# Fused transformer blocks on one core: joined products in a triangular inverse, a reordered tail, and SiLU ahead of a sigmoid

## The chip, the cores and the metric

The kernel runs as one launch on one core of a Trainium2 chip. The metric is the device time of a run in microseconds (us); lower is better. The core has five engines with a queue of instructions each: TensorE (PE in the rows; its weight loads are PEld), VectorE (DVE), ScalarE (ACT), GpSimd (POOL) and SyncE (SP), which here issues the DMAs. Everything is float32, and one matrix product of the program shows as two PE records in the trace. The engines meet only at semaphores that the program sets and waits for by hand.

## The reference, cut to what matters

The input is one sequence of 256 tokens of 1024 channels and 256 context tokens. Two layers of a first network are followed by one block of a second. The change touches only the second block:

```
u  = split(conv(modulate(x), modulate(ctx)) @ w_in)      # mq mk | r k v | mv mo | gates | low ranks
h_m = headnorm(mlstm(silu(mq), silu(mk), mv, gates)) * norm_w;  out_m = sigmoid(mo) * h_m
for t: state = state * w_t - (state @ kh_t) (kh_t a_t)^T + v_t k_t^T;  y_t = state @ r_t     # "wkv", two directions
out_r = (headnorm(y) + bonus) * g
x  = layernorm(ALPHA * x + g1 * ([out_m, out_r] @ w_out))
p  = softmax(h @ rt_g); group = argmax; two best experts of 8 in the group     # h = modulate(x), 32 experts
ffn = sum over the chosen: w * ((silu(h @ ex_gate[e]) * (h @ ex_up[e])) @ ex_down[e])
x  = layernorm(ALPHA * x + g2 * ffn)
```

## The kernel before

The program has six phases: `layers` (the first network), `mid` (projections, convolutions and the mLSTM), `wkv` (the recurrence), `tail` (output product, norms, router), `first` (the first block of an expert) and `pairs` (a loop over pairs of blocks of experts). PSUM has 8 banks. Each phase lists its groups of products in the order in which PE computes them (`wkv_groups`, `tail_groups`, `first_groups`), and the place in that list gives a group its bank and the counts with which `K.full` and `K.empty` are waited for. Each engine runs its queue in the order written in the functions below; nothing is scheduled by a planner.

End of `mid`: ScalarE (`mid_scalar`) takes the square roots of the key norms (L1564), drains the two banks `mo2` through a sigmoid (L1577, by `drain`, L1481), waits for the keys `kh`, and takes SiLU of `km` and `qm` in place (L1583, L1585). PE (`mid_tensor`) computes `mo2`, transposes the gates (L1394) and waits for `km` and `qm` before the first products of the mLSTM loop over four head pairs (`bG`, `qk`, `em`, L1239). That loop's exponentials are L1596 on ScalarE.

`wkv`: the 512 positions (256 of context, then 256 latents) are cut into 8 chunks c of 64; LAT = 4 is the first chunk with an output. Both directions z = 0, 1 run side by side, 8 heads each, as 8 products of 64 rows on the quadrants of the array. Per chunk and direction PE computes three products of the decayed keys (`mr`, `m`, `nr`, in `inner`, by the helper `each`, L1973), turns four operands by products with the identity (`t1`: b and k; `t2`: values and keys, L2001), and inverts a unit triangular matrix in six levels (`level`): a level squares the power and its transpose (`pw`, L2022) and multiplies the inverse by the power (`iv`, L1973). ScalarE copies `pw` (L2109), VectorE adds `iv` to the inverse (`grow`, L2211) and between two levels makes the decayed operands of the next chunk (`hats`, L2147 to L2150). Then come `nv`, `wu` (`solved`), and in the next chunk's turn `gr` (`moved`) and the outputs and state `y`, `st` (`outputs`). GpSimd fills constants for all this after `mid` is done (`wkv_tiles_gpsimd`, L2266, L2268).

`tail`: the output product has two token tiles of two halves of 512 columns, 8 products each: four with the mLSTM's channels, four with the recurrence's, which VectorE delivers one by one (`mixed_r`). `gate_rows(i)` turns a gate vector into rows (8 products L2315, two copies L2400). Per token tile VectorE does two layer norms with square roots on ScalarE (L2407, L2409), PE turns the tile (L2335), ScalarE modulates it (L2416), PE makes the router's logits (L2347), VectorE picks the experts (`route`) with exponentials on ScalarE. When both tiles are routed PE counts places (L2368 to L2379), and VectorE plans blocks of 64 places (`plan`): the number of blocks, the expert of each block (L2593 to L2601, which ends with the semaphore `planned`), and the place of each token.

`first` and `pairs`: the first block's expert is known early; its three matrices are loaded from L2304. `block_count` waits for `planned` and loads the number of blocks into a register. VectorE marks the tokens of the first block (`choose`), PE gathers them (L2667), then gathers the tokens of the next two blocks (L2658), then multiplies the first block with its gate and up matrices (L2681, L2682), turns the hidden rows (L2693), multiplies with the down matrix (L2702) and puts rows back (L2711). The loop over pairs starts at L2723; SyncE loads its weights, three matrices of 2 MB for each block, from `planned` on (L2638).

Of the kernel before, what the change touches and what calls it, by code (L numbers as in the profile page):

```python
# [1078 lines left out]
LAT = T // CH  # L1079


def wkv_groups():
    keys = []
    for c in range(CHUNKS + 1):
# [5 lines left out]
        for z in range(ZS):  # L1090
            if c < CHUNKS:
                keys += [("t1", c, z), ("t2", c, z)]
            if c > LAT:
                keys += [("y", c - 1, z)]
            if 0 < c < CHUNKS:
                keys += [("st", c - 1, z)]
        if c == CHUNKS:
            break
        for n in range(1, LEVELS + 1):
            for z in range(ZS):  # L1100
                if n < LEVELS:
                    keys += [("pw", n, c, z)]
                if n > 1:
# [11 lines left out]
def tail_groups():  # L1115
# [3 lines left out]
    return keys + [("pos", tt) for tt in range(TT)] + [("h2", tt, hf) for tt in range(TT) for hf in range(2)]  # L1119
# [52 lines left out]
CHUNK_EVENTS = dict(wkv_tiles=1, decay=CHUNKS * ZS, hats=CHUNKS * ZS, inv_start=CHUNKS * ZS)  # L1172
# [303 lines left out]
def mid_scalar(act, K):  # L1476
# [94 lines left out]
    key_norms((2, 3))  # L1571
    for i in range(2):
# [9 lines left out]
    act.wait_ge(K.sem["conv_mk"], K.count("conv_mk"))  # L1582
    act.activation(K.km, K.km, ACT.Silu).then_inc(K.sem["km"], 1)  # L1583
    act.wait_ge(K.sem["conv_mq"], K.count("conv_mq"))
    act.activation(K.qm, K.qm, ACT.Silu).then_inc(K.sem["qm"], 1)  # L1585
# [364 lines left out]

def by_pair(bank, n=P):
# [10 lines left out]
def wkv_tensor(pe, K):  # L1962

    one = K.one

# [14 lines left out]
    def inner(c, z):  # L1980
# [3 lines left out]
        kr = t.decayed(c, lat)  # L1984
        each(("mr", c, z), 2 if lat else 1, (t.b, kr))
        each(("m", c, z), 1, (t.decayed(c, False)[:, :, 0, :], t.b))
        each(("nr", c, z), 2 if lat else 1, (t.k, kr))

    def turned(c, z):

        t = K.wkv[z]
        at = chunk_at(c, z)
        v, kr = K.rv[:, :, at:at + CH], t.decayed(c, False)[:, :, 0, :]
        for name, two in (("t1", (t.b, t.k)), ("t2", (v, kr))):
            key = (name, c, z)
            pe.wait_ge(K.empty(key), K.empty_count(key))
            bank = by_two(K.bank(key))
            for i, src in enumerate(two):
                for u in range(HP):
                    for r in HEAD_ROWS:  # L2000
                        ins = pe.matmul(bank[r, u, i, :], src[r, u, :], one[r, :], start=True, stop=True)  # L2001
            ins.then_inc(K.full(key), 1)

    def level(n, c, z):
# [4 lines left out]
        if n == 1:  # L2009
            drained(("mr", c, z), ("m", c, z))  # L2010
        else:
            drained(("pw", n - 1, c, z))
        if n < LEVELS:
# [12 lines left out]
        elif n > 2:  # L2026
# [1251 lines left out]
```

## Time and profile before

| what | value |
|---|---|
| median of 3 runs (lowest, highest) | 2221.85 us (2221.75, 2222.93) |
| the profiled execution: time, span | 2219.88 us, 2218.1 us |
| mean granted TensorE clock | 0.967 of 2.4 GHz |
| busy: PE, DVE, ACT, POOL | 2077.0, 834.1, 480.6, 247.1 us |
| read from memory | 382.54 MB |
| start of `wkv` on PE, start of the output product, start of the loop over pairs | 1406.81, 1647.35, 1755.82 us |

A view of the profile gives times from the start of the span. In a timeline a row merges neighbouring instructions of one line: start, duration, engine, line, operation, operands, count, and in brackets how long the engine was idle before and what ended that. A PE record's duration includes its way through the array, so that neighbours overlap; what a stream of products costs is the distance between starts.

### The profile page before, as it was taken

Reading aid. Unit: us, or ns where it says so; the run is one execution under the profiler, and the core shown is the slowest. Engines: PE = TensorE matmul, PEld = TensorE weight load, DVE = VectorE, ACT = ScalarE, POOL = GpSimd, SP = SyncE. Lnnn points to the kernel's source line nnn. Section 1 sums busy time; section 2 is a strip of 40 time slices with the busy share of each in tenths; the row PEclk is TensorE's granted clock in tenths of the full one; section 3 lists DMA queues with packets and bytes.
Section 4 is the critical chain, followed back from the end, with each engine's and each line's share of the span. In section 5 each row is a group of like instructions: output and inputs, shape, how many; then the busy total and the mean of one; then the engine's idle time right before and its main releaser. Section 6 shows DMA issues by size and latency. Waiting matters only on the chain.

```text
span 2218.1 us, 36982 instructions
## 1 busy us (share of the span) xinstructions
PE 2077.0 (94%) x15231; PEld 1402.7 (63%) x15231; DVE 834.1 (38%) x1551; ACT 480.6 (22%) x868; POOL 247.1 (11%) x229
## 2 busy tenths in 40 slices
PE   8988999999998999999899999899996899999996
PEld 5776868864776777885355555799974444444342
DVE  1388220002248622000358846534446233233324
ACT  2245100000235400000132134443332011101110
POOL 1367000000057600000000001000000000000000
PEclk9999999999999999999899999899996899999998
DMA  7422534443533254444632324300012799999993
GB/s 233 152 76 95 190 120 152 152 153 127 174 120 108 95 190 134 152 153 151 215 109 76 113 92 140 115 4 4 4 43 114 290 372 393 394 412 394 392 393 157
DMA packets 138683, 385.63 MB, mean 174 GB/s; under 512 B 16903, under 2 KB 64367, under 8 KB 127409
## 3 DMA queue, kind: packets, MB, share of 16 engines
q1 hardware_dynamic: 138545, 383.61, 46.8%
q8 instruction: 109, 1.79, 0.3%
q14 instruction: 29, 0.24, 0.0%
HBM read 382.54 MB, written 1.05 MB: 173 GB/s over the span
## 4 chain that ended last, share of the span: by engine, by line
PE 41%; DVE 5%; ACT 2%; issue 1%; DMA 1%; DVEq 0%; POOL 0%; ACTq 0%; POOLq 0%
PE psum L1239 9%; PE psum L2723 9%; PE psum L1973 6%; PE psum L2747 4%; PE psum L2022 3%; PE psum L2658 3%; PE psum L2001 1%; PE psum L2326 1%; PE psum L1438 1%; ACT arena L1596 1%; DVE arena L2931 1%; DVE arena L2858 1%; PE psum L2735 1%; DMA ring<-in_w_ada_dram 1%; PE psum L1254 0%
## 5 line engine op out<-in xcount | busy, mean ns | idle before, releaser
L364 PE MATMUL psum<-arena,ring 128*128 128x256 f32 x1728 | 389.1, 385 | 17.2 <-DVE arena L935 15.8
L364 PEld LDWEIGHTS psum<-arena,ring 128*128 128x128 f32 x1728 | 330.0, 192 | 73.5 <-issue 16.6
L573 PE MATMUL psum<-arena,ring 128*128 128x256 f32 (+1 forms) x1536 | 306.8, 361 | 3.2 <-ACT arena L624 3.2
L573 PEld LDWEIGHTS psum<-arena,ring 128*128 128x128 f32 x1536 | 270.5, 189 | 39.3 <-ACT arena L624 4.0
L624 ACT ACTIVATE arena<-psum 128x512 f32<-128x512 f32 (+2 forms) x116 | 63.0, 568 | 541.1 <-PE psum L573 264.0
L1973 PE MATMUL psum<-arena 64*64 64x64 f32 (+1 forms) x3808 | 149.3, 228 | 6.4 <-DVE arena L2150 3.4
L600 PE MATMUL psum<-ring,arena 128*128 128x512 f32 x352 | 151.4, 592 | 0.0
L1973 PEld LDWEIGHTS psum<-arena 64*64 64x64 f32 x3808 | 139.3, 136 | 8.8 <-issue 3.6
L1239 PE MATMUL psum<-arena,ring 128*128 128x512 f32 (+2 forms) x432 | 142.2, 489 | 0.0
L1013 DVE TENSOR_TENSOR arena<-arena,psum 128x512 f32<-128x512 f32 x22 | 15.2, 690 | 288.8 <-PE psum L573 288.8
L600 PEld LDWEIGHTS psum<-ring,arena 128*128 128x128 f32 x352 | 66.9, 190 | 83.3 <-issue 83.2
L1239 PEld LDWEIGHTS psum<-arena,ring 128*128 128x128 f32 (+1 forms) x432 | 80.6, 187 | 61.4 <-issue 55.8
L2109 ACT ACTIVATE arena<-psum 128x512 f32<-128x512 f32 (+1 forms) x144 | 78.8, 553 | 145.3 <-PE psum L2001 65.1
L2723 PE MATMUL psum<-ring,arena 128*64 128x512 f32 x224 | 100.8, 603 | 4.3 <-DVE arena L2931 3.2
L2724 PE MATMUL psum<-ring,arena 128*64 128x512 f32 x224 | 100.8, 604 | 0.0
L2724 PE MATMUL psum<-arena 128*64 128x512 f32 x224 | 99.4, 595 | 0.0
L2723 PE MATMUL psum<-arena 128*64 128x512 f32 x224 | 99.3, 595 | 0.0
L2903 DVE TENSOR_TENSOR arena<-arena,psum 64x512 f32<-64x512 f32 x28 | 19.0, 679 | 211.9 <-ACT arena L2800 211.9
L1795 DVE SCALAR_TENSOR_TENSOR arena<-psum,arena 128x189 f32<-128x189 f32 (+3 forms) x184 | 80.5, 438 | 21.6 <-ACT arena L1535 13.2
L2800 ACT ACTIVATE arena<-psum 64x512 f32<-64x512 f32 x28 | 16.6, 594 | 310.6 <-PE psum L2724 310.6
L2022 PE MATMUL psum<-arena 64*64 64x64 f32 x2304 | 81.6, 218 | 0.8 <-issue 0.7
L992 DVE SCALAR_TENSOR_TENSOR arena<-arena,psum 128x512 f32<-128x512 f32 x16 | 11.0, 690 | 178.1 <-PE psum L600 135.9
(407 smaller groups left out, 2625.1 us busy)
## 6 DMA issues: line engine op xcount, KB each, us to landing
ring<-in_w_in_dram SPq DMA_DIRECT2D x31, 2048.0 KB, 8.3
ring<-in_ffn_w_dram SPq DMA_DIRECT2D x46, 1024.0 KB, 5.8
arena<-in_ex_gate_dram SPq DMA_DIRECT2D x15, 2048.0 KB, 11.2
arena<-in_ex_up_dram SPq DMA_DIRECT2D x15, 2048.0 KB, 15.7
arena<-in_ex_down_dram SPq DMA_DIRECT2D x15, 2048.0 KB, 17.4
ring<-in_ex_gate_dram SPq DMA_DIRECT2D x14, 2048.0 KB, 10.4
ring<-in_ex_up_dram SPq DMA_DIRECT2D x14, 2048.0 KB, 14.8
ring<-in_ex_down_dram SPq DMA_DIRECT2D x14, 2048.0 KB, 7.7
```

The lines of the kernel that those rows point to most:

```text
L364: ins = pe.matmul(bank[:, j, :], w[:, kc, c * P:(c + 1) * P], moving[:, kc, :], start=kc == 0, stop=kc == k - 1)
L573: ins = pe.matmul(bank[:, j, tokens], both[:, i * DC + kc, j * P:(j + 1) * P], K.xT[:, kc, tokens], start=kc == 0, stop=kc == DC - 1)
L600: ins = pe.matmul(banks[tt, hf], K.hT[:, kc, tt * P:(tt + 1) * P], w[:, i, hf * BANK:(hf + 1) * BANK], start=kc == 0, stop=kc == FC - 1)
L1239: ins = pe.matmul(out, a, b, start=i == 0, stop=i == len(pairs_) - 1)
L1795: last = stt(out=o, in0=i, scalar=w, in1=o, op0=ALU.mult, op1=ALU.add)
L1973: ins = pe.matmul(bank[r, u, :], a[r, u], b[r, u], start=i == 0, stop=i == len(terms) - 1)
L2022: ins = pe.matmul(bank[r, u, i, :], a[r, u], b[r, u], start=True, stop=True)
L2109: act.activation(dst, src, ACT.Copy).then_inc(K.empty(key), 1)
L2658: ins = pe.matmul(bank[:, u * P:(u + 1) * P], K.x_hat[:, tt, kc * P:(kc + 1) * P], K.chosen_at[:, tt, :], start=tt == 0, stop=tt == TT - 1)
L2723: pe.matmul(bank[0:PLACES, :], K.xg[:, kc, mine], up[:, kc, :], start=kc == 0, stop=kc == DC - 1)
L2724: ins = pe.matmul(bank[PLACES:P, :], K.xg[:, kc, mine], gate[:, kc, :], start=kc == 0, stop=kc == DC - 1)
L2747: ins = pe.matmul(bank[hf * PLACES:(hf + 1) * PLACES, :], K.p_hidT[:, j, kc, :], w[:, kc, hf * BANK:(hf + 1) * BANK], start=kc == 0, stop= ...
```

## The change

Five things change.

1. In `mid_scalar` SiLU of `km` and `qm` is taken before the two `mo2` drains, ahead of the wait for `kh`.
2. In `wkv` the values of all chunks are turned once, at the start (`vt`, 4 banks, 64 products), and copied back in place; `t2` is gone. `mr`, `m` and `nr` are products with 128 columns: beside the decayed keys stands the identity, so that the turned b, keys and k come out of the same products, and `t1` remains only for c >= LAT. GpSimd fills two more constants per direction.
3. In levels 2 to 4 (`JOINED`) the product of the power's transpose has power and inverse side by side as moving operand (`pw`, 128 columns), the square of the transpose is a product by itself (`pt`, 64 columns); ScalarE copies `pt`, and VectorE writes power and inverse in one addition of 512 elements per partition.
4. The tail's output product, gates, router counts and plan are reordered.
5. The first block's products with gate and up come before the gather of the next blocks; the experts of the blocks and the router's weights are computed after the first `choose`; `block_count` is read after the first block's work.

```diff
@@ mid_scalar
     key_norms((2, 3))
-    for i in range(2):
-        drain(("mo2", i), ..., ACT.Sigmoid, ...)
...
-    act.wait_ge(K.sem["kh"], K.count("kh"))
     act.wait_ge(K.sem["conv_mk"], K.count("conv_mk"))
     act.activation(K.km, K.km, ACT.Silu).then_inc(K.sem["km"], 1)
     act.wait_ge(K.sem["conv_mq"], K.count("conv_mq"))
     act.activation(K.qm, K.qm, ACT.Silu).then_inc(K.sem["qm"], 1)
+    for i in range(2):
+        drain(("mo2", i), ..., ACT.Sigmoid, ...)
...
+    act.wait_ge(K.sem["kh"], K.count("kh"))
@@ wkv_tensor: inner, level, start
-        kr = t.decayed(c, lat)
-        each(("mr", c, z), 2 if lat else 1, (t.b, kr))
-        each(("m", c, z), 1, (t.decayed(c, False)[:, :, 0, :], t.b))
-        each(("nr", c, z), 2 if lat else 1, (t.k, kr))
+        kr = t.decayed(c, True) if lat else t.decayed_and_one(c)
+        each(("mr", c, z), 2, (t.b, kr))
...
+                ins = pe.matmul(bank[r, u], t.decayed(c, False)[r, u, 0, :], t.b_and_one(u)[r], start=True, stop=True)
...
+        each(("nr", c, z), 2, (t.k, kr))
...
-        if n < LEVELS:
+        if n in JOINED:
+            each(("pt", n, c, z), 1, (z_now, zt_now))
+        elif n < LEVELS:
...
-        if n > 1:
+        if n in JOINED:
+            each(("pw", n, c, z), 2, (zt_now, t.power_and_inv(n - 1)))
+        elif n > 1:
             each(("iv", n, c, z), 1, (zt_now, t.inv))
...
+    pe.wait_ge(K.sem["one_ready"], K.count("one_ready"))
+    for i in range(CHUNKS // 2):
+        values_turned(i)
@@ tail_tensor, after the products
+    for key in (("pos", 0), ("pos", 1), ("total", 0)):
...
+    pe.wait_ge(K.sem["route"], K.count("route", 0, 1))
+    pe.matmul(pos0, K.earlier, K.chosen[:, 0, :], start=True, stop=True)
...
+    pe.wait_ge(K.sem["route"], K.count("route", 0, 2))
+    pe.matmul(total, K.ones, K.chosen[:, 1, :], start=False, stop=True).then_inc(K.full(("total", 0)), 1)
@@ wkv_vector: grow
-        tt_op(t.inv, t.inv, by_pair(K.bank(key), CH), ALU.add).then_inc(K.empty(key), 1)
+        if n in JOINED:
+            ins = tt_op(t.power_and_inv(n), by_two(K.bank(key)), t.zero_and_inv, ALU.add)
+        else:
+            ins = tt_op(t.inv, t.inv, by_pair(K.bank(key), CH), ALU.add)
+        ins.then_inc(K.empty(key), 1)
@@ wkv_tiles_gpsimd
     for t in K.wkv:
+        pool.memset(t.zero, 0.0).then_inc(link.sem, 1)
+        pool.wait_ge(link.sem, link.count())
+        pool.tensor_copy(t.kb_and_one[:, 2 * HP, :], K.one).then_inc(link.sem, 1)
+        pool.wait_ge(link.sem, link.count())
@@ tail_scalar
     head_norm_scalar(act, K, "yv", "y_sq", "y_c", K.eps[:, 1:2], "y_nrm")
+    gate_diagonals(0)
     gate_rows(0)
-    gate_rows(1)
+    gate_diagonals(1)
     for tt in range(TT):
...
+        if tt == 0:
+            gate_rows(1)
@@ route, then route_weights
-    tt_op(K.chosen[:, tt, :], hot1, hot2, ALU.add).then_inc(link.sem, 1)
-    dve.wait_ge(link.sem, link.count())
-
+    tt_op(K.chosen[:, tt, :], hot1, hot2, ALU.add).then_inc(K.sem["route"], 1)
     tt_op(s[:, 1:2], s[:, 2:3], s[:, 4:5], ALU.subtract).then_inc(K.sem["rt_exp"], 1)
+    dve.wait_ge(K.sem["route"], K.count("route", 0, tt + 1))
+
+
+def route_weights(dve, K, link, tt):
...
     dve.wait_ge(K.sem["rt_e2"], K.count("rt_e2", 0, tt + 1))
@@ pair_tensor: these two groups change places
-    pe.wait_ge(K.sem["chosen_at"], K.count("chosen_at"))
-    for q in range(2):
-        pe.wait_ge(K.empty(("first", q)), K.empty_count(("first", q)))
-        gather(q, K.bank(("first", q))).then_inc(K.full(("first", q)), 1)
-
...
     ins.then_inc(K.full(("in1", 0)), 1)
+    pe.wait_ge(K.sem["chosen_at"], K.count("chosen_at"))
+    for q in range(2):
+        pe.wait_ge(K.empty(("first", q)), K.empty_count(("first", q)))
+        gather(q, K.bank(("first", q))).then_inc(K.full(("first", q)), 1)
@@ pair_vector
-    blocks = block_count(dve, K)
     link = Chain(K.place_done)
     choose(dve, K, link, 0, PLACES, "one_chosen")
+    more = Chain(K.dve_done, K.dve_base)
+    owners(dve, K, more)
+    for tt in range(TT):
+        route_weights(dve, K, more, tt)
```

PE's queue at the start of `wkv`, chunk 0: before, the inner products of both directions (L1973), the turned operands (L2001), and the levels (L2022 with L1973).

```order
L1973 MATMUL psum<-arena 64x64 x48
L2001 MATMUL psum<-arena 64x64 x64
L2022 MATMUL psum<-arena 64x64 x32
L1973 MATMUL psum<-arena 64x64 x16
L2022 MATMUL psum<-arena 64x64 x16
```

Now the turned values (L2032) come first, and the inner products (L1990; L2008 is `m`) are 128 columns wide; L2059 is the first level, and the rows from `64x64 x24` on begin with `nv` and hold the joined level 2.

```order
L2032 MATMUL psum<-arena 64x64 x64
L1990 MATMUL psum<-arena 64x128 x8
L2008 MATMUL psum<-arena 64x128 x8
L1990 MATMUL psum<-arena 64x128 x16
L2008 MATMUL psum<-arena 64x128 x8
L1990 MATMUL psum<-arena 64x128 x8
L2059 MATMUL psum<-arena 64x64 x32
L1990 MATMUL psum<-arena 64x64 x24
L1990 MATMUL psum<-arena 64x128 x8
L1990 MATMUL psum<-arena 64x64 x8
```

The 64 turning products of a chunk have left this place, and a joined level is 8 narrow and 8 wide products where it was 24 narrow ones.

PE's queue in the tail before: output products (L2326), gate rows (L2315), turned token tile (L2335), router (L2342, L2347).

```order
L2326 MATMUL psum<-ring,arena 128x512 x16
L2315 MATMUL psum<-arena 128x128 x8
L2326 MATMUL psum<-ring,arena 128x512 x16
L2315 MATMUL psum<-arena 128x128 x8
L2335 MATMUL psum<-arena 128x128 x8
L2342 MATMUL psum<-arena 128x36
L2347 MATMUL psum<-arena 128x36 x8
```

And now, with the output products as L2406, the gate rows as L2395, the turned tile as L2415 and the router as L2422 and L2427:

```order
L2406 MATMUL psum<-ring,arena 128x512 x22
L2395 MATMUL psum<-arena 128x128 x8
L2406 MATMUL psum<-ring,arena 128x512 x10
L2415 MATMUL psum<-arena 128x128 x8
L2422 MATMUL psum<-arena 128x36
L2427 MATMUL psum<-arena 128x36 x8
L2395 MATMUL psum<-arena 128x128 x8
```

The first tile's two halves are complete after 24 of the 32 products, and the second gate's rows have moved behind the first tile's router products.

VectorE's queue in the plan before: the blocks are counted (L2582 to L2589), then the experts of the blocks (L2593 to L2601), then the places (L2603 on).

```order
L2585 SCALAR_TENSOR_TENSOR arena<-psum,arena 128x32 x3
L2587 TENSOR_TENSOR arena<-arena,psum 128x32
L2589 SCALAR_TENSOR_TENSOR arena<-arena 128x32
L2593 TENSOR_TENSOR arena<-arena 128x1280
L2596 COPY arena<-arena 128x1
L2597 TENSOR_REDUCE arena<-arena 128x40
L2599 TENSOR_SCALAR arena<-arena 128x40
L2601 CAST block_expert<-arena 128x41
L2603 TENSOR_TENSOR arena<-arena 128x32
```

In the changed queue the same stretch goes from the blocks to the places at once:

```order
L2680 SCALAR_TENSOR_TENSOR arena<-psum,arena 128x32 x3
L2687 TENSOR_TENSOR arena<-arena,psum 128x32
L2689 SCALAR_TENSOR_TENSOR arena<-arena 128x32
L2692 TENSOR_TENSOR arena<-arena 128x32
L2694 SCALAR_TENSOR_TENSOR arena<-arena,psum 128x32
```

The five instructions for the experts (now L2720 to L2728) stand behind the first `choose` (L2928, L2932).

## Rows read from the trace of the kernel before

**Rows 1.** Stages: length, PE, PEld, DVE, ACT, POOL busy (records), PEclk, DMA share, GB/s.
```profile
1465.00:1495.00 30.00, 29.59 (x954) 29.07 (x952) 10.72 (x26) 12.27 (x24) 0.00 (x0) 1.00 0.02 4
1681.00:1715.00 34.00, 18.36 (x79) 17.04 (x80) 26.24 (x85) 10.55 (x29) 0.00 (x0) 0.50 0.40 160
1719.00:1735.00 16.00, 11.26 (x51) 11.08 (x52) 4.65 (x22) 1.89 (x2) 0.00 (x0) 0.50 0.96 389
1755.00:2205.00 450.00, 425.48 (x2044) 184.06 (x2044) 136.92 (x295) 49.02 (x99) 0.00 (x0) 0.99 0.89 369
```

**Rows 2.** Timeline at the end of the projections, around SiLU.
```profile
1306.30 0.60 ACT L1481 ACTIVATE arena<-psum 128x512 f32<-128x512 f32 x1 [6.67 <-PE psum L1239]
...
1313.59 0.33 DVE L1875 COPY arena<-psum 128x160 f32<-128x160 f32 x1 [4.45 <-PE psum L1394]
...
1318.08 6.04 PE L1239 MATMUL psum<-arena 128*128 128x256 f32 x24 [4.53 <-issue]
1320.21 1.28 ACT L1596 ACT_TABLE_LOAD   x1 [2.23 <-PE psum L1239]
```

**Rows 3.** Timeline at the entry to the recurrence.
```profile
1406.81 1.44 PE L1973 MATMUL psum<-arena 64*64 64x64 f32 x22 [3.42 <-DVE arena L2150]
```

**Rows 4.** Chain that ended last, in the recurrence: start, length, engine, line, records.
```profile
1415.57 1.87 PE psum L2022 x64
...
1539.70 8.16 PE psum L1973 x160
```

**Rows 5.** Timeline of one level in chunk 5.
```profile
1563.55 0.64 PE L1973 MATMUL psum<-arena 64*64 64x64 f32 x16
...
1564.30 0.42 DVE L2211 TENSOR_TENSOR arena<-arena,psum 128x256 f32<-128x256 f32 x1 [0.98 <-PE psum L1973]
```

**Rows 6.** Timeline of the tail's output product and norms.
```profile
1647.35 13.89 PE L2326 MATMUL psum<-ring,arena 128*128 128x512 f32 x32
...
1670.00 0.69 DVE L2491 TENSOR_TENSOR arena<-psum,arena 128x512 f32<-128x512 f32 x1 [1.26 <-PE psum L2326]
...
1676.60 1.95 PE L2315 MATMUL psum<-arena 128*128 128x128 f32 x16
...
1678.58 0.60 ACT L2400 ACTIVATE arena<-psum 128x512 f32<-128x512 f32 x1 [0.30 <-PE psum L2315]
...
1679.30 0.16 DVE L2435 RECIPROCAL arena<-arena 128x1 f32<-128x1 f32 x1 [6.72 <-ACT arena L2407]
...
1685.39 1.94 PE L2335 MATMUL psum<-arena 128*128 128x128 f32 x8 [6.84 <-issue]
...
1690.22 0.16 DVE L2435 RECIPROCAL arena<-arena 128x1 f32<-128x1 f32 x1 [0.27 <-ACT arena L2407]
```

**Rows 7.** Timeline of routing and planning.
```profile
1698.97 3.63 PE L2347 MATMUL psum<-arena 128*128 128x36 f32 x16 [0.17 <-ACT arena L2416]
...
1707.30 0.20 DVE L2558 TENSOR_TENSOR arena<-arena 128x32 f32<-128x32 f32 x1
...
1711.99 0.19 DVE L2582 TENSOR_SCALAR arena<-psum 128x32 f32<-128x32 f32 x1 [3.10 <-PE psum L2378]
...
1713.38 1.49 DVE L2593 TENSOR_TENSOR arena<-arena 128x1280 f32<-128x1280 f32 x1
...
1716.81 0.18 DVE L2603 TENSOR_TENSOR arena<-arena 128x32 f32<-128x32 f32 x1
...
1721.45 0.42 DVE L2823 TENSOR_SCALAR arena<-arena 128x64 f32<-128x64 f32 x2 [0.98 <-DVE arena L2621]
...
1722.44 7.09 PE L2667 MATMUL psum<-arena 128*128 128x64 f32 x32 [7.11 <-DVE arena L2827]
```

**Rows 8.** The chain that ended last, in the first block.
```profile
1730.82 6.08 PE psum L2658 x32
...
1746.65 3.66 PE psum L2702 x16
```

**Rows 9.** Timeline where the loop over pairs starts.
```profile
1755.82 0.94 PE L2723 MATMUL psum<-ring,arena 128*64 128x512 f32 x1 [1.02 <-DVE arena L2891]
```

More of the change, by code:

```diff
@@ L1079 @@
 LAT = T // CH
+JOINED = range(2, LEVELS - 1)
 def wkv_groups():
-    keys = []
+    keys = [("vt", i) for i in range(CHUNKS // 2)]
     for c in range(CHUNKS + 1):
@@ L1100, in wkv_groups @@
             for z in range(ZS):
+                if n in JOINED:
+                    keys += [("pt", n, c, z)]
                 if n < LEVELS:
                     keys += [("pw", n, c, z)]
-                if n > 1:
+                if n > 1 and n not in JOINED:
                     keys += [("iv", n, c, z)]
@@ L1118, in tail_groups @@
     keys += [("h2T", 0), ("h2T", 1), None, None, ("rt", 0), ("h2T", 2), ("h2T", 3), ("rt", 1)]
-    return keys + [("pos", tt) for tt in range(TT)] + [("h2", tt, hf) for tt in range(TT) for hf in range(2)]
+    return keys + [("pos", tt) for tt in range(TT)] + [("total", 0)] + [("h2", tt, hf) for tt in range(TT) for hf in range(2)]
 def tail_closes():
@@ L2055, in outputs @@
         t = K.wkv[z]
[L2056 removed]
+        u0, vt = t.wu[:, :, 1, :], values_at(c, z)
         if c > 0:
@@ L2085, in wkv_tensor @@
             if n == 1:
+                if c == 0:
+                    for i in range(CHUNKS // 2):
+                        drained(("vt", i))
                 for z in range(ZS):
@@ L2584, in plan @@
     for k in range(1, T // PLACES):
-        stt(out=blocks, in0=total, scalar=float(k * PLACES), in1=blocks, op0=ALU.is_gt, op1=ALU.add).then_inc(link.sem, 1)
-        dve.wait_ge(link.sem, link.count())
+        ins = stt(out=blocks, in0=total, scalar=float(k * PLACES), in1=blocks, op0=ALU.is_gt, op1=ALU.add)
+        if k < T // PLACES - 1:
+            ins.then_inc(link.sem, 1)
+            dve.wait_ge(link.sem, link.count())
+        else:
+            ins.then_inc(K.empty(("total", 0)), 1)
+            dve.wait_ge(K.empty(("total", 0)), K.drained_count(("total", 0)))
     tt_op(blocks, blocks, its, ALU.subtract).then_inc(link.sem, 1)
@@ L2622, in plan, with owners @@
             dve.wait_ge(link.sem, link.count())
+def owners(dve, K, link):
+    tt_op, ts_op = dve.tensor_tensor, dve.tensor_scalar
+    ends = K.plan[:, 1, :]
+    n = 2 * PAIRS
+    tt_op(K.ended, K.token[:, 0:n].unsqueeze(2).broadcast_to([P, n, EXPERTS]), ends.unsqueeze(1).broadcast_to([P, n, EXPERTS]),
+          ALU.is_ge).then_inc(link.sem, 1)
+    dve.wait_ge(link.sem, link.count())
+    dve.tensor_copy(K.owner[:, n:n + 1], ends[:, EXPERTS - 1:EXPERTS])
+    dve.tensor_reduce(K.owner[:, 0:n], K.ended, AX_X, ALU.add).then_inc(link.sem, 1)
+    dve.wait_ge(link.sem, link.count())
+    ts_op(K.owner[:, 0:n], K.owner[:, 0:n], float(EXPERTS - 1), None, ALU.min).then_inc(link.sem, 1)
+    dve.wait_ge(link.sem, link.count())
+    dve.tensor_copy(K.block_expert[:, 0:n + 1], K.owner[:, 0:n + 1]).then_inc(K.sem["planned"], 1)
 def pair_sync(sp, K, A):
@@ L2895, in pair_vector @@
     assert link.n == FIRST_LINKS, link.n
+    blocks = block_count(dve, K)
     with dve.Fori(0, PAIRS) as i, dve.If(i * 2 < blocks):
```

230 lines of the change are left out of this document (142 added, 88 removed).

## The prediction

> **What bounds the kernel now.** I read the table of stages first. The loop over pairs keeps PE busy for 425.5 of 450 us [rows 1] and isn't touched, so whatever happens ahead of it shifts it as a block, if its first weights are there in time. In the recurrence PE works 29.6 of 30 us, VectorE 10.7, the DMAs nothing: there the columns of the products set the time. From 1681 to 1715 PE is busy for 18.4 of 34 us, VectorE for 26.2, and the granted clock is 0.50, the 1.2 GHz level: a chain of short steps, bound by who waits for whom. Second, the timelines of the four joints (SiLU, entry, tail, plan); third, the chain of waits for what one stream of products costs. I sum against the profiled execution, 2219.9 us, which is 2.0 below the median of the runs; the result is put back on the median at the end.
>
> **SiLU first.** ScalarE idles 6.67 us before the first sigmoid drain [rows 2]; SiLU (behind `km` and `qm`, whose convolutions VectorE has long made) fits there. Today PE waits 4.53 us before L1239 at 1318.08; then it can go on right behind the transposed gates, which VectorE starts to copy at 1313.59. The exponentials' table load comes 2.13 us after PE's start at the low clock and takes 1.28 (1320.21 + 1.28 = 1321.5). PE has not stopped by then in the new order, so I take half of the 2.13: 1313.6 + 1.1 + 1.28 = 1316.0, **−5.5**; with the low clock, 1317.0, −4.5. The sigmoids come after SiLU, before the table load, and are done by then. The mLSTM loop is a chain of PE and ScalarE without a DMA, so the shift goes through.
>
> **Columns in the recurrence.** 64 records of 64 columns take 1.87 us, 29.2 ns each, so a narrow product 58.3 ns; 160 records, of which 32 are narrow, take 8.16: (8.16 − 0.93) / 128 = 56.5 ns, a wide product 113 ns [rows 4]. Per direction, inner products and turned operands: chunks 0 to 3 had 56 narrow (3.27 us), now 24 wide (2.71); chunks 4 to 7 had 16 wide and 40 narrow (4.14), now 24 wide and 16 narrow (3.65): 8 × −0.56 + 8 × −0.49 = −8.4. A joined level had 24 narrow (1.40), now 8 narrow and 8 wide (1.37): 48 × −0.03 = −1.4. Sum **−9.8**. 7136 records become 5728. If a wide product were two narrow ones (116.6 ns), the saving would be 7.5; since the inner products come to the array's quadrants in another order, I also allow −11.
>
> The Trainium skill ("TensorE: Matmul & The Clock Gate", Back-to-back issue gap) says that a product with few columns is held by issue, and with hardware decode off by about 62 ns of the sequencer for each MATMUL. By that the 7136 records would take 442 us, and 704 products fewer would bring far more than the columns. The trace has 29.2 ns a record and 236 us for the phase, so no such floor is seen here.
>
> **Entry.** `vt` is 64 narrow products, 3.7 us at full clock, 6.7 at the low one. They need only the values, and PE idles 3.42 us there [rows 3]. GpSimd fills two more constants for each direction; priced like VectorE's 256 elements, 0.42 [rows 5], and partly ahead of time, the keys come ~1.2 us later. The first inner product then starts some 2.4 us after 1406.81, but those 64 products are already counted out of the chunks, and PE has raised its clock sooner by its work (the first chunk ran partly at the low level). Net **+0.3**, near the lower end because PE's idle time covers the late keys (−0.8 to +2.3).
>
> **Longer steps in the levels.** VectorE's addition took 0.42 us for 256 elements, and takes 0.69 for 512 [rows 5, 6]. A level's last product is issued at 1563.55 + 16 × 0.029 = 1564.02, and VectorE starts at 1564.30: 0.28; back to PE ~0.1. One direction's step from its products to the next level's operands is now 1.37 + 0.28 + 0.69 + 0.10 = 2.44; PE has both directions' products to do meanwhile, 2.74. Slack 0.3: covered, except where VectorE makes the decayed operands between levels 3 and 5 (1.0 to 1.4 us a piece). I take 0.3 in each of chunks 0 to 2 and 0.7 in each of 3 to 6: **+3.6** (0 to +8).
>
> **The output product and the norms.** 32 products take 1647.35 to 1676.60 less one gate of 1.95: 27.3 us, 0.43 for each record [rows 6]. The first tile's halves are now complete behind 46 and 48 records and a gate: 1668.9 and 1669.7, instead of beside the first 32. VectorE needs 2.17 a half (L2491 and two more), 0.4 for the variance and 0.3 for the root: the reciprocal comes at ~1674.1 instead of 1679.30, where it stood behind the second gate's copy (L2400, 1678.58) on ScalarE. So the tile is turned at 1680.2 (before 1685.39), and its router products end at 1686.5. Now the new wait: PE computes the second gate's rows only then (1.95 x 16 records at full, ~3.6 us at the low clock), and ScalarE's two copies of them stand ahead of the second tile's square root. Bank 2 is there at 1690.1, copied at 1691.0, reciprocal at 1691.3; VectorE had the variance at ~1684.8 and waits. Before: 1690.22. So 5 us gained on the first tile end in a queue: **+0.5**, rounded down for a clock between (−0.9 with the clock up, +1.1).
>
> **Route and plan.** From the router's end (1698.97 + 3.63) to the last choice (L2558, ends 1707.50) nothing changes but ~0.1. Then places were counted 4.5 us later (VectorE starts at 1711.99) [rows 7]. Now PE has done the first tile's counts before and needs one product for `total`: VectorE starts at ~1708.3. From there to the gather it was 10.45 us, of which 1716.81 − 1713.38 = 3.43 for the blocks' experts and 0.98 for reading the register go. So 14.94 becomes 0.8 + 6.04 = 6.9: **−8.0** (−7.0 if ScalarE's copies of the token tiles, done about 1 us ahead by my count, are late). What is late next: `planned`. It goes behind the first `choose` and five instructions, so comes some 3.5 us after the gather's start instead of 5.5 before it. In the shifted frame this is 1 us later. The first block's weights of the pair, 389 GB/s over 16 us [rows 1], land ~16 us after, some 10 us before the loop: no cost.
>
> **First block.** Before, from the first gather to L2702: 24.2 us = 7.1 + 1.3 wait + 6.08 gather (clock low) + 9.75 [rows 7, 8]. The 9.75 are 16 products with gate and up, 7.0 us (16 records of L2702's shape take 3.66, 0.44 a pair), and 2.7 for SiLU, product and turning. Now: 7.1 + 0.75 (copy) + 9.5 (7.0 and some low clock at the start) + 3.8 for the gather at the full clock, under which SiLU and the product hide + 1.6 turning = 22.75: **−1.5** (−5.8 with the clock up throughout, +0.5 with it low for longer). The register load on PE now stands behind the last rows put back, where PE waited 1.02 us for VectorE anyway [rows 9]: **+0.3** (0 to +1.0, the load's 0.98 [rows 7]).
>
> **The sum.** −5.5 − 9.8 + 0.3 + 3.6 + 0.5 − 8.0 − 1.5 + 0.3 = −20.1. Profiled 2199.8; on the median 2221.85 − 20.1 = **2201.8**.
>
> **The rivals.**
> - *The clock stays up* through the second gate and the first block, since the gaps there are shorter. Against it: 0.50 over all of 1681 to 1715 [rows 1]. −5.8 instead of −1.5, −0.9 instead of +0.5, and 1.6 in turning and routing both tiles: 2221.85 − 20.1 − 4.3 − 1.4 − 1.6 = 2194.5.
> - *VectorE paces the joined levels.* If hand-overs cost 0.4 us more than I count, each of the 24 level pairs waits 0.4: +9.6, 2211.4. For it: 0.69 against 0.42 on a slack of 0.3; against it: VectorE is busy for a third.
> - *The stream of weights sets the start of the loop.* `planned` is 1 us later in the shifted frame, and DMA busy for 0.96 of its stretch. If the loop's first products wait for the second block's matrices, the first block's and plan's gain of 9.5 is lost: 2211. Against it: the last wait at 1755.82 is VectorE's.
> - *Slower:* VectorE's joined addition reads one operand from PSUM and two strided pieces. L2491 says 0.69 us for PSUM and 512 elements [rows 6]. The slack covers it up to 2.74 − 1.37 − 0.38 = 0.99 us; at 2.0, each of 24 steps costs 1.01 more, 24 us against a gain of 20: 2226. From 0.99 + 20.1 / 24 = 1.83 us on the gain is gone.
>
> **Chances.** Forecast 0.60, clock 0.14, VectorE 0.12, stream 0.07, slower 0.05, and 0.02 for an outcome within 0.2%, which is about what a measurement can tell from no change. The forecast's own range is 2197 to 2207; the rivals on both sides widen it to 2191 to 2212. Faster 0.93, within 0.2% 0.02, slower 0.05.
>
> **What would show it.** The exponentials start near 1316 (a 1321 would refute the first term). Output product 11.4 us earlier, near 1636; a phase from `vt` to there that isn't shorter by about 6 refutes the columns, and PE idle for more than 10 us before the products of the levels speaks for VectorE. First tile's reciprocal 5 us earlier in its frame, the second's within 1 us. From the router's last product to the gather 11.8 us instead of 19.8. The loop starts at ~1735.7, and an iteration is as long as before. Wrong altogether it is if ScalarE's queue, not PE, turns out to hold the recurrence, where it copies `pt` now and nothing in my rows prices it.

## The result, and where the time went

The changed kernel takes 2192.84 us in the median of 4 runs (2191.62 to 2197.73), the kernel before 2221.8 (2218.06 to 2222.93, 4 runs): 29.0 us less, ratio 0.9877, 95% interval 0.9858 to 0.9896. Forecast: 2201.8, range 2191.0 to 2212.0. The sign and the range held; the forecast's own range, 2197 to 2207, didn't. The lower end of the wide range stood for a clock rival that didn't happen, so that the time lies inside it is partly luck.

The two profiled executions (2219.88 and 2192.70 us) differ by 27.2 us, 1.8 less than the medians, because the kernel before was profiled in a run 1.9 us under its median. Cut at the same events in both traces:

| stretch | before | after | difference | predicted |
|---|---|---|---|---|
| start to the transposed gates (nothing changed) | 1313.1 | 1314.3 | +1.2 | 0 |
| gates to the first exponential | 8.4 | 2.9 | −5.5 | −5.5 |
| to the last product of the mLSTM phase (end) | 81.9 | 83.0 | +1.1 | 0 |
| entry and recurrence | 239.7 | 227.5 | −12.2 | −5.9 |
| to the output product | 4.3 | 4.5 | +0.3 | 0 |
| output product to second tile's reciprocal | 42.9 | 43.6 | +0.7 | +0.5 |
| to the first gather | 32.2 | 24.3 | −7.9 | −8.0 |
| gather to the first down product | 24.2 | 22.5 | −1.7 | −1.5 |
| to the loop over pairs | 9.2 | 9.2 | 0.0 | +0.3 |
| loop to the end | 462.3 | 459.2 | −3.1 | 0 |

Five terms came out within 0.3 us of their own stretch. The miss of 7 us in the traces (9.0 on the medians) is 6.3 us in the recurrence and 3.1 in the loop over pairs, whose code is unchanged, less 2.3 by which the start and the loop over head pairs, also unchanged, took longer. The 1.1 us of the latter are not by chance: see u_silu. These are the stages of the changed kernel (length, PE, PEld, DVE, ACT, POOL busy with their records, granted clock, DMA share, GB/s); the first answers to the recurrence of [rows 1], the fourth to its stretch at the low clock.

```profile
1465.00:1495.00 30.00, 29.81 (x760) 29.48 (x758) 15.06 (x31) 12.38 (x32) 0.00 (x0) 1.00 0.02 4
...
1660.00:1680.00 20.00, 11.35 (x46) 9.35 (x44) 13.08 (x21) 4.39 (x12) 0.00 (x0) 0.71 0.00 1
1680.00:1690.00 10.00, 7.98 (x34) 7.39 (x34) 7.10 (x36) 4.77 (x13) 0.00 (x0) 0.50 0.28 92
1690.00:1710.00 20.00, 13.85 (x59) 11.90 (x61) 14.88 (x65) 5.97 (x9) 0.00 (x0) 0.50 0.83 338
1710.00:1735.00 25.00, 22.63 (x106) 10.43 (x104) 7.52 (x17) 2.33 (x5) 0.00 (x0) 0.94 1.01 430
```

PE is busy for 29.81 of 30 us in the recurrence, before 29.59: the longer steps on VectorE (15.06 us busy instead of 10.72) left PE no idler. And these 30 us hold fewer records, 760 instead of 954, because more of them are wide.

The timeline of the changed kernel at SiLU, for [rows 2]: SiLU (L1577, L1579) fits ScalarE's idle time, PE goes on 0.4 us after it began to transpose the gates, and the table load follows PE's start by 1.24 us, where I had 1.1.

```profile
1300.80 1.91 ACT L1577 ACTIVATE arena<-arena 128x2048 f32<-128x2048 f32 x1
1302.62 1.04 ACT L1579 ACTIVATE arena<-arena 128x1024 f32<-128x1024 f32 x1
...
1314.27 0.44 PE L1398 MATMUL psum<-arena 40*128 40x40 f32 x4
...
1314.64 4.94 PE L1243 MATMUL psum<-arena 128*128 128x256 f32 x32
...
1315.88 1.28 ACT L1600 ACT_TABLE_LOAD   x1 [0.90 <-PE psum L1243]
```

The entry, for [rows 3]: the 64 turning products (128 records) take 6.24 us, the first 5.1 of them at the low clock (up to 1405.6), and the decayed operands are ready (L2215, 1404.62) before PE is done with them. The inner products start at once.

```profile
1400.55 6.24 PE L2032 MATMUL psum<-arena 64*64 64x64 f32 x128 [0.36 <-ACT arena L1485]
...
1404.62 0.69 DVE L2215 TENSOR_TENSOR arena<-arena 128x512 f32<-128x512 f32 x1
...
1406.61 1.06 PE L1990 MATMUL psum<-arena 64*64 64x128 f32 x16
```

The chain that ended last in the recurrence (start, length, engine, line, records), for [rows 4]. The 224 records of one chunk's joined levels and `nv`, 128 narrow and 96 wide, take 8.98 us without a gap: (8.98 − 128 × 0.0292) / 96 = 54.6 ns a wide record. Only behind the joined levels does the chain pass through VectorE, for 0.43 us.

```profile
1437.30 8.98 PE psum L1990 x224
1446.29 0.47 PE psum L2059 x16
1446.75 0.47 PE psum L1990 x16
1447.22 0.66 PE psum L2059 x16
1447.88 0.47 PE psum L1990 x16
1448.35 0.12 issue
1448.46 0.69 PE psum L1990 x16
...
1449.25 0.43 DVE arena L2284
```

The tail, for [rows 6]. The first reciprocal comes 26.9 us behind the start of the output product (before 32.0), the second 43.6 behind it (before 42.9): ScalarE's copies of the second gate (L2487) stand ahead of the second root (L2495), VectorE idles 6.06 us.

```profile
1632.23 19.04 PE L2406 MATMUL psum<-ring,arena 128*128 128x512 f32 x44
...
1659.09 0.16 DVE L2525 RECIPROCAL arena<-arena 128x1 f32<-128x1 f32 x1 [0.27 <-ACT arena L2495]
...
1671.29 3.76 PE L2395 MATMUL psum<-arena 128*128 128x128 f32 x16
...
1673.38 0.60 ACT L2487 ACTIVATE arena<-psum 128x512 f32<-128x512 f32 x1 [4.18 <-PE psum L2395]
1675.09 0.60 ACT L2487 ACTIVATE arena<-psum 128x512 f32<-128x512 f32 x1 [1.11 <-PE psum L2395]
1675.58 0.19 ACT L2495 ACTIVATE arena<-arena 128x1 f32<-128x1 f32 x1
...
1675.81 0.16 DVE L2525 RECIPROCAL arena<-arena 128x1 f32<-128x1 f32 x1 [6.06 <-ACT arena L2495]
```

Routing, plan and first block, for [rows 7, 8]: the blocks are counted at 1693.80, 0.8 us behind the last choice (L2648, before 4.5), and the experts (L2720) stand behind the `choose` (L2932) that the gather (L2772) waits for. The next gather (L2763) runs at the full clock in 3.84 us, before 6.08.

```profile
1692.77 0.19 DVE L2648 TENSOR_TENSOR arena<-arena 128x32 f32<-128x32 f32 x1
...
1693.80 0.19 DVE L2677 TENSOR_SCALAR arena<-psum 128x32 f32<-128x32 f32 x1 [0.76 <-PE psum L2465]
...
1699.36 0.48 DVE L2932 SCALAR_TENSOR_TENSOR arena<-arena 128x64 f32<-128x64 f32 x2
1699.76 1.49 DVE L2720 TENSOR_TENSOR arena<-arena 128x1280 f32<-128x1280 f32 x1
...
1700.10 7.06 PE L2772 MATMUL psum<-arena 128*128 128x64 f32 x32 [2.55 <-DVE arena L2932]
...
1717.36 3.84 PE L2763 MATMUL psum<-arena 128*128 128x128 f32 x32
```

### The profile page after: what moved, and what is told of

It is laid out like the page before. It is cut to its first block, busy times and chain, and to the rows that moved or that the text cites. A ratio compares the mean times of both kernels' runs of the same rounds, so it can differ in the third digit from the quotient of the medians.

```text
span 2190.9 us, 34184 instructions
## 1 busy us (share of the span) xinstructions
PE 2066.7 (94%) x13823; PEld 1392.1 (64%) x13823; DVE 847.5 (39%) x1551; ACT 469.8 (21%) x880; POOL 248.0 (11%) x233
## 3 DMA queue, kind: packets, MB, share of 16 engines
HBM read 382.54 MB, written 1.05 MB: 175 GB/s over the span
## 4 chain that ended last, share of the span: by engine, by line
PE 42%; DVE 4%; ACT 2%; issue 1%; DMA 1%; DVEq 0%; ACTq 0%
PE psum L1243 9%; PE psum L2828 9%; PE psum L1990 8%; PE psum L2852 5%; PE psum L2763 3%; PE psum L1442 1%; PE psum L2406 1%; ACT arena L1600 1%; PE psum L2059 1%; DVE arena L3041 1%; DVE arena L2963 1%; PE psum L2840 1%; PE psum L2008 1%; DMA ring<-in_w_ada_dram 1%; PE psum L1265 1%
## 5 line engine op out<-in xcount | busy, mean ns | idle before, releaser
L364 PE MATMUL psum<-arena,ring 128*128 128x256 f32 x1728 | 389.3, 385 | 17.2 <-DVE arena L935 15.9
L1990 PE MATMUL psum<-arena 64*64 64x64 f32 (+1 forms) x4320 | 179.9, 237 | 3.1 <-issue 1.9
L1990 PEld LDWEIGHTS psum<-arena 64*64 64x64 f32 x4320 | 171.7, 134 | 5.1 <-issue 3.1
L2159 ACT ACTIVATE arena<-psum 128x256 f32<-128x256 f32 (+1 forms) x156 | 68.4, 446 | 141.9 <-PE psum L1990 53.3
L2828 PEld LDWEIGHTS psum<-ring,arena 128*64 128x64 f32 x224 | 29.5, 137 | 70.9 <-issue 70.9
## 6 DMA issues: line engine op xcount, KB each, us to landing
ring<-in_ex_gate_dram SPq DMA_DIRECT2D x14, 2048.0 KB, 10.5
```

Source lines behind the costliest of these rows:

```text
L364: ins = pe.matmul(bank[:, j, :], w[:, kc, c * P:(c + 1) * P], moving[:, kc, :], start=kc == 0, stop=kc == k - 1)
L1990: ins = pe.matmul(bank[r, u, :], a[r, u], b[r, u], start=i == 0, stop=i == len(terms) - 1)
L2159: act.activation(dst, src, ACT.Copy).then_inc(K.empty(key), 1)
L2828: pe.matmul(bank[0:PLACES, :], K.xg[:, kc, mine], up[:, kc, :], start=kc == 0, stop=kc == DC - 1)
```

## The experiments

Eleven runs were made, one of them the kernel before once more; the last three are told of at the end. The changed kernel is their starting point unless said otherwise. The ratios to the kernel before have 95% intervals of about ±0.0018, 4 us, as wide as most effects sought; so each verdict rests on distances within the trace, and the time stands beside it. Such distances repeat closely where the clock does: from the first inner product to the tail the changed kernel and eight others with the same recurrence all took 221.1 us. The medians come from four series of runs, in which the kernel before itself had 2221.8, 2219.97, 2217.83 and 2220.03 us, so a difference of medians can be off by as much as 4 us (u_tail is 1.2 us faster than the changed kernel by the medians, and 0.4 slower by the ratios).

| run | edit | ratio to before | median us |
|---|---|---|---|
| (changed kernel) | | 0.9877 | 2192.84 |
| u_silu | SiLU back | 0.9894 | 2196.19 |
| u_joined | no joined level | 0.9893 | 2195.16 |
| dose | one more VectorE copy a joined level | 0.9890 | 2194.43 |
| u_plan | experts back in the plan | 0.9894 | 2195.70 |
| u_first | first block's order back | 0.9899 | 2195.27 |
| u_tail | tail's order back | 0.9879 | 2191.61 |
| root_first | second gate's copies behind the root | 0.9859 | 2186.95 |
| old_order | the same, old product order | 0.9842 | 2183.46 |

**u_silu**

```
     key_norms((2, 3))
-    (SiLU of km and qm)
     for i in range(2):
         drain(("mo2", i), ..., ACT.Sigmoid, ...)
...
     act.wait_ge(K.sem["kh"], K.count("kh"))
+    (SiLU of km and qm)
```

> The changed kernel with SiLU of km and qm back behind the two sigmoid drains and the wait for kh. Theory (prediction's first term): PE waits about 4.5 us for SiLU again, the exponentials start 5.5 us later counted from the transposed gates, and all of it reaches the end: 5.5 us slower than the changed kernel. Rival: the loop over head pairs has slack of its own or another clock, since in the changed kernel's trace the loop's end had kept only 3.2 of the 4.3 us by which it began earlier; then 3.2 to 4.3 us slower.

From the transposed gates to the first exponential 8.4 us again instead of 2.9: the 5.5 are shown. But they don't all arrive. To the first inner product it is 96.2 us from the gates, and in the changed kernel 92.3: 3.8 us, 3.4 in the medians. The rival holds, and the trace shows where the rest goes. These are the 64 records of one product group (L1442) in the first head pair, in the changed kernel and in u_silu, and between them the clock of the changed kernel:

```profile
1323.44 8.83 PE L1442 MATMUL psum<-arena 128*64 128x256 f32 x64 [2.00 <-ACTq L1605]
...
1323.71:1327.12 3.41, 3.41 (x20) 1.91 (x18) 1.29 (x2) 0.83 (x2) 0.32 (x1) 0.50 1.04 399
...
1328.54 7.16 PE L1442 MATMUL psum<-arena 128*64 128x256 f32 x64 [0.68 <-ACTq L1605]
```

With the late SiLU the clock is low from 1316.7 to 1323.5, and 5.6 of these 6.8 us lie ahead of the first exponential (1322.28), so the 8.4 us hold them already; these products run at the full clock. With the early one a low stretch of 3.4 us begins after PE's idle 2.0 us, in the middle of these products, and costs 1.7: from the first exponential of the first head pair to that of the second it is 17.2 us instead of 15.5, in all ten kernels with the early SiLU. The rest varies with the clock at the end of the phase: of these ten kernels, four reach the first inner product 91.1 us behind the gates, with 3.4 us of low clock ahead of the recurrence, and six after 92.3 to 92.4, with 10.2 us of it as in u_silu. So like is compared with like above.

**u_joined**

```
-JOINED = range(2, LEVELS - 1)
+JOINED = range(0)
```

> The changed kernel with no joined level (JOINED empty): levels 2 to 4 as before, turned values and 128-column inner products kept. Theory of the prediction: the levels lose 1.4 us of columns and give back 3.6 us of waits for the longer addition, so this kernel is 2.2 us faster than the changed one. Rival, from the changed kernel's trace (a joined level of one direction every 1.34 us, against 1.40, and no more idle PE than before): nothing is waited for, and this kernel is 48 x 0.06 = 2.9 us slower, or a bit more.

From the first inner product to the first product of the tail 222.25 us instead of 221.08: joined levels gain, 1.2 us. Neither number held. (The whole trace is 2.4 us longer, as the loop over pairs took 1.6 more, see the last runs.) The chunk periods (distance between the second directions' L2215, chunks 1 to 7) say why:

```
before    25.54 26.92 28.72 28.58 32.33 32.20
u_joined  23.45 25.37 25.75 27.52 31.25 31.14
changed   23.38 25.28 25.57 27.45 31.07 31.07
```

The joining gives 0.07 to 0.18 us a chunk where its columns give 192 × 0.0292 − 96 × 0.0546 = 0.36: the rest goes into waits behind the joined levels. This is the same stretch of the chain (end of chunk 1) in u_joined, where PE goes on without VectorE:

```profile
1446.35 0.47 PE psum L2059 x16
1446.81 0.47 PE psum L1990 x16
1447.28 0.47 PE psum L2059 x16
1447.75 0.47 PE psum L1990 x16
1448.21 0.04 issue
```

**dose**

```
         if n in JOINED:
+            dve.tensor_copy(t.spare, t.zero)
             ins = tt_op(t.power_and_inv(n), by_two(K.bank(key)), t.zero_and_inv, ALU.add)
```

> The changed kernel with one more VectorE copy of 256 elements (about 0.4 us, of zeros into a spare tile) ahead of each of the 48 joined additions. By the prediction's accounting a step of one direction is 1.34 + 0.28 + 0.69 + 0.10 = 2.41 us against 2.68 us of products of both directions, slack 0.27; with the copy it is 2.83, each of 24 steps waits 0.15 us: 3.6 us slower. Rival A: VectorE already paces the levels, then each step waits all of 0.42: 10 us slower. Rival B: the hand-overs overlap more than counted: less than 1 us.

The copy took 0.29 us, not 0.42, and in the middle of the levels it costs nothing: the additions (L2283) follow each other by 1.34 us as in the changed kernel.

```profile
1443.53 0.29 DVE L2282 COPY arena<-arena 128x256 f32<-128x256 f32 x1 [0.45 <-PE psum L1990]
1443.74 0.68 DVE L2283 TENSOR_TENSOR arena<-psum,arena 128x512 f32<-128x512 f32 x1
...
1444.87 0.30 DVE L2282 COPY arena<-arena 128x256 f32<-128x256 f32 x1 [0.45 <-PE psum L1990]
1445.08 0.69 DVE L2283 TENSOR_TENSOR arena<-psum,arena 128x512 f32<-128x512 f32 x1
...
1446.01 0.69 DVE L2215 TENSOR_TENSOR arena<-arena 128x512 f32<-128x512 f32 x1
...
1446.82 0.68 DVE L2283 TENSOR_TENSOR arena<-psum,arena 128x512 f32<-128x512 f32 x1
```

Behind the decayed operands (L2215) the next addition comes 1.74 us after the last, in the changed kernel 1.55. The stretch from inner products to tail grew by 2.5 us, a chunk by 0.20 to 0.74. Rival A falls (48 × 0.29 / 2 = 7.0 would have been due), and rival B too. The forecast had 3.6, but its reason doesn't carry the 2.5: with 0.29 us the accounting gives 0.02 a step, 0.5 in all. In this stretch VectorE is short only where it also makes the decayed operands.

**root_first**

```
         act.activation(..., ACT.Sqrt).then_inc(K.sem["x4_std"], 1)
+        if tt == 1:
+            gate_rows(1)
...
-        if tt == 0:
-            gate_rows(1)
```

> The changed kernel with ScalarE's two copies of the second gate's rows moved behind the second token tile's second square root; PE's order is unchanged. Theory (the tail's term: the second root is late only because it queues behind these copies): VectorE's reciprocal for the second tile comes at its variance + 0.6 us, 5.6 us earlier, and the kernel ends 5.6 us earlier, about 2187. Rival: the next wait takes its place (ScalarE's modulation of the second tile or the banks of the gate rows, which the turned tile needs): 0 to 2 us.

Timeline of ScalarE and VectorE: the second root at once behind the variance, the second reciprocal 37.8 us behind the output product instead of 43.6, 5.8 earlier.

```profile
1668.49 0.20 ACT L2495 ACTIVATE arena<-arena 128x1 f32<-128x1 f32 x1 [0.58 <-DVE arena L2544]
...
1668.73 0.17 DVE L2525 RECIPROCAL arena<-arena 128x1 f32<-128x1 f32 x1 [0.27 <-ACT arena L2495]
```

The first gather comes 61.3 us behind the output product instead of 67.9, the medians differ by 5.9. The theory holds: no next wait took its place.

**old_order** (beside the edit above; the new order's lines, which these replace, and the waits are left out)

```
+    for tt in range(TT):
+        for hf in range(2):
+            out_product(tt, hf, range(DC // 2))
+    gate_rows(0)
+    for tt in range(TT):
+        for hf in range(2):
+            out_product(tt, hf, range(DC // 2, DC)).then_inc(K.full(("out2", tt, hf)), 1)
```

> ScalarE's copies of the second gate behind the second square root of the second tile (as in the run before), and besides the output product in its old order (first halves of all four banks, the first gate's rows, then tile 0 before tile 1). Theory: with the root no longer queued behind copies, only the completion of the first tile's banks counts, and in the old order VectorE had its variance 25.2 us after the start of the output product against 26.5 now: the first reciprocal, the gather and the end come 1.2 to 1.3 us earlier than with the new order, about 2185.7. Rival: PE is idle for longer ahead of the turned tile and its clock falls earlier; then nothing is gained, or 1 to 2 us lost.

First reciprocal 25.5 us behind the start of the output product (root_first 26.9), the second 36.4 (37.8): 1.35 earlier. Up to the gather 0.6 is left of it (60.7 against 61.3): root_first's clock was 0.63 in 1668 to 1676 and 0.59 in 1676 to 1684, where this run had 0.50 in both, the rival's price. It has the lowest median seen: 2183.46 us (2182.35 to 2185.68, 5 runs), ratio 0.9842, interval 0.9829 to 0.9856. Against root_first's 0.9859 (0.9843 to 0.9876) the new product order shows no gain once the root is freed; that the old one is better in the end is not shown either, since the intervals overlap.

**u_tail** (both tail engines in the old order)

> The changed kernel with the tail's output product, both gates' rows and ScalarE's copies in the order of the kernel before; plan and first block stay changed. Theory (tail's term, +0.5 predicted, +0.7 in the trace): the first reciprocal comes 5 us later, the second 0.7 us earlier, and the kernel ends 0.5 to 0.7 us earlier, so this half of the reordering brought nothing. Rival: the clock, which idle PE in the old order lets fall, costs it 1 to 2 us later on.

First reciprocal 32.0, second 42.9 us behind the output product, gather at 67.2 instead of 67.9. The theory holds: the tail's reordering as made costs 0.7 us in the trace (medians 1.2), because what it gave the first tile was queued away from the second. The rival doesn't show: from the output product on the granted clock is 0.72 over 80 us in both.

**u_plan** (`owners` called ahead of the places)

> The changed kernel with the five instructions for the blocks' experts back in the plan, ahead of the places; the router's weights stay behind the first choose. Theory: they take 3.4 us on VectorE's path, the first gather and the end come 3.4 us later. Rival: the first gather is held by ScalarE's copies of the token tiles, which end about 2 us ahead of it, and then part of the 3.4 was never a gain; or the earlier weights of the first pair give time back in the loop: 0 to 2 us slower.

Second reciprocal to first gather 27.7 us instead of 24.3: 3.4, as by the theory. Up to the loop 0.7 comes back, in the first block, where the clock was 0.74 instead of 0.72 and PE got through the same products in 20.4 instead of 21.2 us; the medians differ by 2.9.

**u_first** (the gather of the next blocks ahead of L2781 again)

> The changed kernel with the gather of the next two blocks ahead of the first block's products with gate and up again. Theory (first block's term): that gather runs at the low clock in front of them, 6.08 us instead of 3.8, and VectorE's wait of 1.3 us ahead of it comes back: the distance from the first gather to L2806 goes from 22.5 to 24.2, end 1.7 us later. Rival: what counts is when the clock rises, and PE's work raises it at the same time in either order: then 0 to 0.5 us.

From the first gather to L2806 22.8 us instead of 22.5: only 0.4. But the clocks differ, and already ahead of the edit: here the first 1.0 us of the gather ran at the full clock (6.18 us instead of 7.06), and the low clock ended 1.5 us sooner, counted from the gather. The stretch from the gather to L2806, before, changed and in u_first (the first two numbers behind the window are its length and PE's busy time, the third from the end is the granted clock):

```profile
1722.44:1746.65 24.21, 21.23 (x103) 15.72 (x103) 4.22 (x16) 3.34 (x6) 0.00 (x0) 0.73 0.60 240
...
1700.10:1722.56 22.46, 21.20 (x103) 14.27 (x103) 8.63 (x29) 3.34 (x6) 0.00 (x0) 0.72 0.85 349
...
1699.05:1721.87 22.82, 19.83 (x102) 14.31 (x103) 8.60 (x29) 3.34 (x6) 0.00 (x0) 0.78 0.83 337
```

PE is idle for 3.0 us before, 1.3 in the changed kernel and 3.0 again in u_first: the order of the two groups is worth 1.7 us of idle time, as by the theory. In u_first 1.4 of it is hidden by the clock, which gets PE through the same products in 19.8 instead of 21.2 us. The two kernels compared at the start had nearly the same clock here (0.73 and 0.72) and the same busy time, so their −1.7 is not the clock's. The medians differ by 2.4.

**before_again, shift1, shift4.** The first is the kernel before, the others are old_order with

```
+    for _ in range(1):               # 4 in shift4
+        pe.wait_ge(K.sem["planned"], K.count("planned"))
     blocks = block_count(pe, K)
```

> The kernel before, once more, for its trace. If the 3.1 us that the changed kernel saved from the start of the loop over pairs to the end lie in the program, the loop again takes 462.3 us to the end, with 1.7 us of low clock in its first iteration and 0.11 us more per iteration than the changed kernel. If the clock decides by chance, the 1.7 us move or vanish here, and only the 0.11 us per iteration stay.

> The kernel old_order with one satisfied wait more on PE ahead of the read of the number of blocks, so that PE's loop stands one instruction further on. If the place of the loop's code decides the 0.11 us per iteration (the joined levels taken out or put in change only what PE has ahead of the loop, and the iteration changed by 0.11 us), an iteration changes by 0.1 us or more in this run or in the next, 1.5 us in all. Rival: the place doesn't matter, both loops take 427.8 us from first to last product.

> As the run before, with four satisfied waits more on PE. By the theory of the code's place an iteration differs from 31.43 us by 0.1 us in one of the two runs; by its rival in neither.

In before_again (2219.13 us, one run) the loop takes 460.6 us to the end instead of 462.3: the low clock in the loop's first iteration (0.57 from 1756 to 1760 in the first trace) is not there, clock 1.00. So 1.7 of the 3.1 us are the clock's chance. The other 1.4 stay: first to last product of the loop 429.2, with the joined levels 427.8 to 427.9 (in dose 429.6, where a first iteration at a clock of 0.94 takes 1.8 more). An iteration is 31.53 us in all kernels with the joined levels, 31.63 in the kernel before and 31.64 in u_joined, which has 429.4 (not 31.43, as in what was expected of shift4). shift1 (2186.85 us) and shift4 (2184.11) have 427.8 both: moving PE's loop by one and by four instructions changes nothing. Larger moves, and moves of the other engines' loops, are not tested, and u_joined has 768 more matmul records ahead of PE's loop than the changed kernel, the kernel before 1408. The extra 0.11 us doesn't even stand in one place: in the kernel before, PE starts L2747 0.29 us after it fell idle behind ScalarE's copy, in the changed one 0.18, with the same instructions; in u_joined it is 0.18 too, but PE idles 0.37 instead of 0.26 us at the top of the iteration. Why is open.

## Why the prediction was right or wrong

- *SiLU*: the exponentials came 5.5 us earlier as forecast, but "the shift goes through" is wrong. 1.7 us are lost in the first head pair, where the low stretch of the clock now falls on PE's work instead of on its wait. With what the phase's end gave back, 4.4 of the 5.5 reach the end of the phase in the two traces, and 3.8 the first inner product against u_silu. The sum had 0 for this.
- *What bounds it, route and plan, first block, register load*: the terms are right to 0.3 us against the trace. u_plan shows the largest part of route and plan when taken back alone, u_first the first block's in PE's idle time; and the parts of the first block came as counted (from the gather to the first products 7.8 us, 9.5 for them, 3.84 for the next gather).
- *Tail*: right, mechanism and price (+0.5, measured +0.7); u_tail and root_first show both sides of it.
- *Columns in the recurrence*: this term of the sum was mis-sized. I took a wide record for 56.5 ns from 160 records in 8.16 us [rows 4]; the gapless stretch after gives 54.6. The kernels exchange 2816 narrow for 1280 wide records: −82.2 + 69.9 = −12.3 instead of −9.8. The row was one of `L1973` alone and wasn't without a wait: its first wide product stands 0.16 us ahead of the next, the others 0.11; the excess was 0.24 us over 128 records, but it is multiplied by 1280. PE's busy time at full clock went from 227.3 to 216.8 us, 10.5 less, and the first 4.6 us, which the kernel before ran at a clock of 0.51, are worth 2.3 at the full one: 12.8.
- *Longer steps in the levels*: the step that failed. I added 3.6 us of waits and left the waits of the kernel before standing. The new waits are there, as u_joined and dose show, but half as long: of the joining's 2.9 us of columns only 1.2 arrive, so 1.7 are waits. And 2.4 us of the old ones are gone. u_joined, with none of the new waits, has periods 1.06 to 1.08 us below those of before from chunk 4 on, where columns alone (96 narrow less, 32 wide more) give 1.05; but 2.1, 1.6 and 3.0 below ahead of that, where columns give 1.3. PE's idle time there went from 0.55, 0.18 and 1.0 to 0.04 us each; the rest shows in the distances between the starts of the records, which a record's long duration hides: over 29.2 and 54.6 ns a record these were 1.55, 0.75 and 2.43 us too long, and are 0.61, 0.65 and 0.69. Why these old waits went no run separates; they are marked "issue", with nothing in the profile that PE waited for, and they wander: in before_again the three periods are 24.99, 27.44 and 28.72. A rival nobody tested is late code: the queue that loads instructions moved 57 packets, 0.93 MB, over the recurrence before, and 45, 0.74 MB, over the changed one. Whether the waits are its doing is not shown.
- *Entry*: I expected the first inner product 2.4 us later in its frame and 2.1 of it given back by the clock. It came 3.0 later (3.4 to 6.4 us behind the last product of the phase before), and the 4.5 us at the low clock that the kernel before had in its first chunk are gone, 2.2 us: +0.8 instead of +0.3.
- *The recurrence together*: 3.0 more ahead of the first inner product, −12.3 of columns, −2.2 of clock, +1.7 of new waits and −2.4 of old ones make −12.2. The old waits are what is left over once the others are taken off; u_joined against the kernel before leaves the same 2.4. Against the forecast of −5.9 the columns account for 2.5, the new waits for 1.9, the old for 2.4, and the entry for −0.5.
- *The rivals*: the clock was low through the second gate (up to 1675.3) and again from 1678.7 to 1712.8, so the clock rival didn't happen; the stream of weights didn't hold the loop's start (PE's last wait there, 1.03 us, is VectorE's); VectorE doesn't pace the levels (dose); the joined addition takes 0.69 us, so the slower case was out.
- The sum came out 7.1 us short in the traces: recurrence 6.3, loop 3.1 (1.7 of it clock, 1.4 open), head-pair loop −1.1 by SiLU's clock, start −1.2, small ones 0.

## What to carry to other kernels

A price per instruction that multiplies by a thousand has to come from a stretch in the chain that is gapless and made of one kind, or it carries someone's wait. When work is brought forward, look at the in-order queue behind it on every engine it touches: here five microseconds gained for one tile ended in front of the other tile's square root, and moving two copies behind that root gave 5.8 us, where the reordering of the output product by itself had cost 0.7. When a shift is to go through a chain, look where the low stretches of the clock lie: here one fell on a wait before and on work after. And in a stretch where PE is nearly always busy, a change of the instruction mix changes the old waits too; both sets have to be priced.

## Seen beside it

- The loop over head pairs, with the same code, took from the gates to the first inner product 91.1 us in four kernels and 92.3 to 92.4 in six; the granted clock from 1319 to the phase's end was 0.95 in the changed kernel and 0.98 in u_plan, which was 1.3 us shorter. One trace is not enough to see an effect of 1 us behind it.
- The loop over pairs runs at one of two paces 0.11 us an iteration apart in kernels whose loop is the same instruction for instruction.
